# SSM loops with fill work by halves, and the attention's output projection begun behind the last chunk

## The reference, cut to what matters

```python
seg = a_t[..., :, None] - a_t[..., None, :]
decay = jnp.exp(jnp.where(tril, seg, -jnp.inf))
cb = jnp.einsum('bclgn,bcsgn->bcgls', cm, bm)
y_diag = jnp.einsum('bcgls,bcghls,bcsghp->bclghp', cb, decay, xdt)
chunk_states = jnp.einsum('bclgn,bclgh,bclghp->bcghpn', bm, decay_to_end, xdt)
_, prev = lax.scan(carry_step, init, (chunk_states, chunk_decay))   # state before each chunk
y_off = jnp.einsum('bclgn,bcghpn,bclgh->bclghp', cm, prev, jnp.exp(a_cum))
...
y = y + xs * d_skip;  y = y * silu(z);  y = normalize(y per group) * ssm_norm_g
branch_att = att @ w_o_att
branch_ssd = y @ w_o_ssd
merged = sigmoid(g_att) * branch_att + sigmoid(g_ssd) * branch_ssd
return merged @ w_out
```

## Time and profile before

| | us |
|---|---|
| median of 3 runs | 2543.91 (2539.17 to 2546.9) |
| the profiled execution | 2542.98 |
| its span in the profile | 2541.3 |
| TensorE busy in it | 2383.3 |
| TensorE's mean granted clock, share of full | 0.979 |

### The profile page before, as it was taken

The page is one execution under the profiler, slowest core; times in us unless marked ns, Lnnn a source line. Parts: engine busy times, 40 slices in busy tenths (PEclk is TensorE's granted clock), DMA queues, the critical chain, the costliest instruction groups (busy, mean ns, idle before and its releaser), DMA issues.

```text
span 2541.3 us, 31932 instructions
## 1 busy us (share of the span) xinstructions
PE 2383.3 (94%) x12062; PEld 1950.0 (77%) x12062; DVE 1371.9 (54%) x1971; ACT 724.1 (28%) x1371; POOL 858.5 (34%) x353
## 2 busy tenths in 40 slices
PE   3999999997998999999999799999799999999997
PEld 3966878874656888888877688888688888888885
DVE  4249999964656266574655565654523232232316
ACT  5153121005651233434255210024511121211112
POOL 1221332216771352533444233335222333332221
PEclk9999999998999999999999899999999999999998
DMA  7110342216652113131230533333211111111103
GB/s 260 34 34 34 111 171 99 91 42 203 198 174 71 34 59 125 39 120 59 68 107 22 215 136 108 124 132 136 81 50 50 50 50 50 39 43 50 50 33 132
DMA packets 145737, 233.92 MB, mean 92 GB/s; under 512 B 8068, under 2 KB 111844, under 8 KB 144612
## 3 DMA queue, kind: packets, MB, share of 16 engines
q1 hardware_dynamic: 121952, 173.45, 21.0%
q10 hardware_dynamic: 23684, 59.06, 6.0%
HBM read 180.06 MB, written 52.43 MB: 91 GB/s over the span
## 4 chain that ended last, share of the span: by engine, by line
PE 85%; DVE 8%; ACT 3%; issue 2%; DMA 1%; POOL 0%; ACTq 0%; SPq 0%; DVEq 0%
PE ps L634 83%; DVE c_out L1799 2%; PE ps L838 1%; DVE probT L1742 1%; DVE mod_sum L1587 1%; DVE c_out L1797 0%; DMA ada_raw<-in_ada_w_dram 0%; PE ps L921 0%; DVE c_out L1801 0%; DVE x_tm L1969 0%; DVE zy L1845 0%; DMA x_d<-x_tm 0%; ACT decay L1437 0%; DVE x_tm L1906 0%; ACT zy L1370 0%
## 5 line engine op out<-in xcount | busy, mean ns | idle before, releaser
L634 PE MATMUL ps<-a_hi,w_hi 128*128 128x512 f32 x1728 | 679.7, 393 | 11.5 <-DVE a_lo L1852 5.6
L634 PE MATMUL ps<-a_lo,w_hi 128*128 128x512 f32 x1728 | 675.2, 391 | 0.0
L568 POOL CAST w_hi<-raw 128x2048 fp32r<-128x2048 f32 x90 | 176.3, 1959 | 1326.5 <-PE ps L634 1014.4
L634 PE MATMUL ps<-a_hi,w_lo 128*128 128x512 f32 x1728 | 545.0, 391 | 0.0
L570 POOL TENSOR_TENSOR w_lo<-raw,w_hi 128x2048 fp32r<-128x2048 f32 x90 | 429.9, 4777 | 7.2
L1931 DVE TENSOR_TENSOR x_tm<-x_tm,ps 128x1024 f32<-128x1024 f32 x120 | 146.5, 1221 | 453.1 <-PE ps L634 453.1
L634 PEld LDWEIGHTS ps<-a_hi,w_hi 128*128 128x128 f32 x1728 | 326.6, 189 | 81.7 <-issue 7.8
L634 PEld LDWEIGHTS ps<-a_lo,w_hi 128*128 128x128 f32 x1728 | 326.5, 189 | 67.7 <-issue 0.7
L634 PEld LDWEIGHTS ps<-a_hi,w_lo 128*128 128x128 f32 x1728 | 325.7, 188 | 68.2
L634 PE MATMUL ps<-w_hi,a_hi 128*128 128x256 f32 (+1 forms) x896 | 259.6, 290 | 5.0 <-ACT row L1488 2.0
L634 PE MATMUL ps<-w_lo,a_hi 128*128 128x256 f32 (+1 forms) x896 | 254.7, 284 | 0.0
(11 more groups left out here) (249 smaller groups left out, 3162.9 us busy)
## 6 DMA issues: line engine op xcount, KB each, us to landing
raw<-in_w_in_dram SPq DMA_DIRECT2D x35, 1024.0 KB, 5.3
ada_raw<-in_ada_w_dram SPq DMA_DIRECT2D x16, 1024.0 KB, 8.8
raw<-in_w_up_dram SPq DMA_DIRECT2D x16, 1024.0 KB, 5.7
raw<-in_w_down_dram SPq DMA_DIRECT2D x16, 1024.0 KB, 4.9
gates<-gate_d SPq DMA_DIRECT2D x12, 1024.0 KB, 5.0
act_raw<-acts_d ACTq DMA_DIRECT2D x20, 512.0 KB, 5.8
ada<-in_ada_w_dram SPq DMA_DIRECT2D x8, 1024.0 KB, 20.5
acts_d<-decay ACTq DMA_DIRECT2D x16, 512.0 KB, 2.6
```

The source lines that it names most:

```text
L568: nc.gpsimd.tensor_copy(hi, src).then_inc(hi_made, 1)
L634: return nc.tensor.matmul(o, a, b, start=start, stop=stop)
```

## The change

The fill work is placed by halves. `fill_parts(g, k)` gives the halves behind chunk `k`: two behind chunks 0 to 5 and one behind 6 and 7 in group 0; two behind chunks 0 to 3 and one behind 4 to 7 in groups 1 and 2; two behind chunks 0 to 5 and none behind 6 and 7 in group 3. In every group one half now stands between `segments(0)` and `segments(1)`, and one behind `segments(1)`. The state product of each group's last chunk is left out; `mix_done` of that chunk comes from the product `state, c_fm`.

The first output block moves ahead of the four turns of y in the last group. It ends in banks 5, 0, 1 and 2 (`FIRST_OUT`), and the turns use the pairs 3-4 and 6-7. The buffers `act_raw`, `gates` and `gated` get other addresses, so that SP can load the attention tiles 0 and 1 as soon as the last `segments` is done, and tiles 2 and 3 when the last fill tiles are stored. ScalarE rounds tiles 0 to 3 inside the last loop and tiles 4 to 7 behind the root, ahead of the copies of the turned y; DVE makes `a_lo` of tiles 0 and 1 ahead of y of the last chunk, 2 and 3 behind it, 4 behind the variance, and 5 to 7 behind the 8 scalings. POOL's split of the next weight block waits for the last y and no longer for the scalings. `acc` is cleared in two parts, and DVE's loop over the first two turns of output blocks is written out. SP's load of `x_in` waits for other semaphores.

```diff
-    act_raw = [place(f"act_raw{i}", [P, SEQ], F32, R2 + (0, 4, 48, 52)[i] * K) for i in range(4)]
-    gates = [place(f"gates{i}", [P, 2, SEQ], F32, R2 + (8 + 8 * i) * K) for i in range(2)]
-    gated = [place(f"gated{i}", [P, 512], F32, R2 + (24 + 2 * i) * K) for i in range(2)]
+    act_raw = [place(f"act_raw{i}", [P, SEQ], F32, R2 + (12352, 16448, 0, 4128)[i]) for i in range(4)]
+    gates = [place(f"gates{i}", [P, 2, SEQ], F32, R2 + (48 * K, 20544)[i]) for i in range(2)]
+    gated = [place(f"gated{i}", [P, 512], F32, R2 + 8256 + 2 * i * K) for i in range(2)]
...
-        def fill_places(g):
-
-            return {k: k for k in range(NT)} if g == 0 else {0: 2, 1: 3, 3: 4, 4: 5, 5: 6, 6: 7}
+        def fill_parts(g, k):
+
+            first = 2 if g == 0 else 4
+            each = (2, 2, 2, 2, 2, 2, 1, 1) if g == 0 else (2, 2, 2, 2, 1, 1, 1, 1) if g + 1 < NG else (2, 2, 2, 2, 2, 2, 0, 0)
+            n = first + sum(each[0:k])
+            return range(n, n + each[k])
...
+        FIRST_OUT = (5, 0, 1, 2)
...
                 load(N_O + j, cols(w_o_att[0], j * WC))
                 if j == 1:
 
+                    sp.wait_ge(seg_done, NG * NT)
+                    for k in range(4):
+                        if k >= 2:
+                            sp.wait_ge(fill_stored[k - 2], 64 * NG)
+                        sp.dma_start(act_raw[k][:, :], acts_d[k]).then_inc(act_in[k], 16)
+
                     sp.wait_ge(y_ready, NG * NT)
-                    for b in range(2):
-                        sp.wait_ge(fill_stored[b], 64 * NG)
-                    for k in range(4):
-                        sp.dma_start(act_raw[k][:, :], acts_d[k]).then_inc(act_in[k], 16)
-
-                    for m in range(2):
-                        sp.wait_ge(y_stored[m], 16 * 2 * NG)
                     load_gates(0, 0)
                     load_gates(1, 2)
...
-                    sp.wait_ge(gate_used, 16 * 3)
-                    sp.wait_ge(act_split, 3 * KT)
+                    sp.wait_ge(act_split, 4 * KT - 1)
...
-            pool.wait_ge(gn_ready, NG * NT)
+            pool.wait_ge(y_ready, NG * NT)
             with pool.Fori(0, (N_ALL - N_O) // 2 - 1) as i:
...
+            def y_banks(g, f):
+                return (4, 6)[f % 2] if g + 1 < NG else (3, 6)[f % 2]
...
+                j = 1 if g else 0
                 segments(0)
+                fill(g, j, 0)
                 segments(1)
-                if g:
-                    fill(g, 1, 0)
-                    fill(g, 1, 1)
+                fill(g, j, 1)
                 pe.wait_ge(tile_out, g * 5 + 5)
-                places = fill_places(g)
...
-                        mm(ps[:, 3, :], c_fm[:, k * P:(k + 1) * P], state[:, :, :].rearrange("p h d -> p (h d)"),
-                           start=True, stop=True)
-                    mm(ps[:, 6, :], b_tm[:, k, :], xde[k % 2][:, :, :].rearrange("p h d -> p (h d)"),
-                       start=True, stop=True).then_inc(mix_done, 1)
+                        mixed = mm(ps[:, 3, :], c_fm[:, k * P:(k + 1) * P], state[:, :, :].rearrange("p h d -> p (h d)"),
+                                   start=True, stop=True)
+                        if k == NT - 1:
+                            mixed.then_inc(mix_done, 1)
+                    if k < NT - 1:
+                        mm(ps[:, 6, :], b_tm[:, k, :], xde[k % 2][:, :, :].rearrange("p h d -> p (h d)"),
+                           start=True, stop=True).then_inc(mix_done, 1)
                     if k + 2 < NT:
                         segments(k + 2)
-                    if k in places:
-                        fill(g, places[k], 0)
-                        fill(g, places[k], 1)
-
-            for f in range(4):
-                y_turn(NG - 1, f)
+                    for part in fill_parts(g, k):
+                        fill(g, *divmod(part, 2))
...
-                last = fm_block(n, j % 2, extra=0 if turn is None else turn * 2, act_ready=ready, act_used=used)
+                last = fm_block(n, j % 2, extra=0 if turn is None else turn * 2, act_ready=ready, act_used=used,
+                                banks=FIRST_OUT if (o, j) == (0, 0) else None)
                 last.then_inc(w_used[n % 2], 1)
 
-            for j in range(4):
+            pe.wait_ge(decay_done, NG * NT)
+            pe.wait_ge(fill_out, NG * 8)
+            pe.wait_ge(y_ready, NG * NT - 1)
+            out_block(N_O, 0, 0)
+            for f in range(4):
+                y_turn(NG - 1, f)
+            pe.wait_ge(yt_out, NG * 4)
+            pe.wait_ge(gate_used, 1)
+            for j in range(1, 4):
                 out_block(N_O + j, j, 0)
...
+            def act_load(k, tile):
+                act.dma_start(act_raw[k % 4][:, :], acts_d[bass.ds(tile, 1)].rearrange("a p s -> p (a s)")).then_inc(act_in[k % 4], 16)
+
+            def first_acts(tiles):
+                for k in tiles:
+                    act.wait_ge(act_in[k % 4], 16 * (k // 4 + 1))
+                    nc.scalar.copy(a_hi[:, k, :], act_raw[k % 4][:, :]).then_inc(hi_copied, 1)
+                    if 1 <= k < KT - 3:
+                        act.wait_ge(act_split, k)
+                        act_load(k + 3, k + 3)
...
                 def squares_of(k):
                     act.wait_ge(y_ready, g * NT + (k + 1))
-                    nc.scalar.activation(c_out[k % 2][:, 0:DG], zy[:, k, :], ACT.Square,
+                    nc.scalar.activation(c_out[0][:, k % 2 * DG:k % 2 * DG + DG], zy[:, k, :], ACT.Square,
...
-                    if k == 1 and g:
-                        fill_evac(g, 1)
-                    if k - 2 in places:
-                        fill_evac(g, places[k - 2])
+                    if k == 1:
+                        fill_evac(g, 1 if g else 0)
+                    for part in fill_parts(g, k - 2) if k >= 2 else ():
+                        if part % 2:
+                            fill_evac(g, part // 2)
+                    if g == NG - 1 and k >= NT - 1:
+                        first_acts({NT - 1: (0, 1), NT: (2,), NT + 1: (3,)}[k])
                     if k >= 2:
                         squares_of(k - 2)
                 act.wait_ge(gn_var, g + 1)
                 nc.scalar.activation(stat[:, 96:104], stat[:, 96:104], ACT.Sqrt).then_inc(gn_root, 1)
+            first_acts(range(4, KT))
             for f in range(4):
                 y_evac(NG - 1, f)
...
                 for k in range(NT):
                     if k + 1 < NT:
                         mix_in(k + 1)
+                    if g == NG - 1 and k == NT - 1:
+                        act_lo(0, tiles=(0, 1))
                     dve.wait_ge(mix_done, g * NT + (k + 1))
...
+                if g == NG - 1:
+                    act_lo(0, tiles=(2, 3))
                 dve.wait_ge(gn_squares, g * NT + NT)
                 ve.tensor_scalar(stat[:, 96:104], stat[:, 96:104], 1.0 / DG, EPS, ALU.mult, ALU.add).then_inc(gn_var, 1)
+                if g == NG - 1:
+                    act_lo(0, tiles=(4,))
...
 
+            act_lo(0, tiles=range(5, KT))
+            V.link(ve.memset(acc[:, 0:KT // 2, :], 0.0))
+            for i in range(2):
                 for j in range(3):
-                    gate_block(N_O + j, j, i)
+                    gate_block(N_O + j, j, i, FIRST_OUT if (i, j) == (0, 0) else None)
+                    if (i, j) == (0, 0):
+                        dve.wait_ge(yt_done, NG * 4)
+                        V.link(ve.memset(acc[:, KT // 2:KT, :], 0.0))
                 act_lo(i * 8 + 8)
                 gate_block(N_O + 3, 3, i)
-                V.leave(2)
```

More of the change, by code:

```diff
@@ L634, in mm, with fm_block @@
                 return nc.tensor.matmul(o, a, b, start=start, stop=stop)
-            def fm_block(n, group, extra=0, act_ready=None, act_used=None):
+            def fm_block(n, group, extra=0, act_ready=None, act_used=None, banks=None):
                 s = n % 2
+                banks = banks or range(4 * group, 4 * group + 4)
                 w_wait(n, extra)
@@ L646, in fm_block @@
                         for q in range(2):
-                            o = ps[:, 4 * group + 2 * m + q, :]
+                            o = ps[:, banks[2 * m + q], :]
                             r = slice(q * 512, q * 512 + 512)
@@ L651, in fm_block @@
                         for q in range(2):
-                            last = mm(ps[:, 4 * group + 2 * m + q, :], wl, a_hi[:, k, q * 512:q * 512 + 512],
+                            last = mm(ps[:, banks[2 * m + q], :], wl, a_hi[:, k, q * 512:q * 512 + 512],
                                       stop=(k == KT - 1))
@@ L857, in y_turn @@
                 for t in range(NT):
-                    last = nc.tensor.transpose(ps[:, 4 + 2 * (f % 2) + t // 4, (t % 4) * P:(t % 4 + 1) * P],
+                    last = nc.tensor.transpose(ps[:, y_banks(g, f) + t // 4, (t % 4) * P:(t % 4 + 1) * P],
                                                zy[:, t, f * P:(f + 1) * P], ident[:, :])
@@ L1447, in _ @@
```

(22 more changed lines are left out.)

10 lines of the change are left out of this document (3 added, 7 removed).

## The result

The median of the changed kernel is 2502.8 us (2501.4 to 2504.7), against 2542.7 for the kernel before: 0.984 of it, with a 95% interval of 0.9826 to 0.986. The forecast was 2504.5. In the profiled executions the span fell from 2541.3 to 2501.8 us, by 39.5, against a sum of 39.6.

A forecast was written before the change was run, and what follows sets the result against it. TensorE, busy 2383.3 of 2541.3 us, was taken as the bound, through its waits and low clock. Terms 11.2 + 6.8 - 2.3 + 3.4 + 3.5 + 11 + 6 = 39.6 us gave 2504.5 us, range 2495 to 2525.

The forecast's parts named there:

- The half ahead of `segments(1)`: Half a fill tile in each group's 4.1 us gap while ScalarE's exponentials finish: 4 x 2.8 = 11.2 us gained.
- The rest waits: What stays of each group's 3.0 us wait for the exponentials once the gap holds a half: 1.0 us each.
- Chunk 2's waits: Three waits for y behind chunk 2 of groups 1 to 3, covered by two halves there: 6.8 us gained.
- New wait behind chunk 4: Groups 1 and 2, where one half doesn't cover y held by POOL's split: 1.2 us each, 2.3 us lost.
- Rival 3: DVE bounds the loop: POOL's subtraction delays all ten singly covered chunks, kernel slower, 2553 us; chance 0.04.
- Last state products: Leaving out the state product of each group's last chunk on TensorE: 4 x 0.86 = 3.4 us gained.
- `turn_tile`: Its waits for DVE's convolutions go, as a half behind the last chunk in groups 1 and 2 gives lead: 3.5 us gained.
- The clock: TensorE's half-clock stretches behind waits mostly go: 11 us gained of 17.5, bounds 0 and 17.5.
- rival 1: The clock doesn't come back: remaining short waits in groups and tail are followed by half clock too, 2520 us; chance 0.18.
- The tail: From chunk 5's end in group 3 to the second output block, first block ahead of the turns: 6 us (5.9) gained.
- TensorE waits 2.3 and 1.8 us: First output block: two waits ahead of tiles 4 and 5, from POOL's subtraction holding DVE's `a_lo` and then the scalings.
- Rival 2: First output block starves, each tile a load late through ScalarE's list: tail -10 instead of +6, 2520.5 us; chance 0.13.

The follow-up runs named there:

- the moved half: Changed kernel with POOL's split behind the scalings and two more turned-tile buffers, one half of group 3's fill put behind chunk 6 instead of 5: 2498.3 us, 0.9810.

## Why the prediction was right, point by point

The groups' lengths can be closed with the prediction's own terms; the clock is what remains.

- **The half ahead of `segments(1)`**: 2.95 us each inside the gap of 4.1, as said (11.2 forecast, 11.8 measured). The rest waits came to 4.0 us for the forecast 4 x 1.0, three of them 0.7 or 0.8 and one, in group 3, 1.8. Chunk 0 was nowhere late.
- **Chunk 2's waits**: 6.8 forecast, 6.8 gone. **New wait behind chunk 4**: 1.2 forecast, 0.92 measured, twice; no other chunk with single cover waited. Rival 3 needed 4 us in each of ten chunks and is refuted.
- **Last state products**: 0.86 each forecast; 0.9 to 1.0 where they were put back. **`turn_tile`**: 3.5 forecast, 3.3 gained, and the wait returns as soon as chunk 7 has no fill.
- **The clock** was the term with the widest bounds (0 to 17.5, taken at 11), and it was under-sized. What it gave back is a remainder here. Group 0 gained 7.9 us: 2.95 is the half, 0.9 the product, 4.1 remain. Group 1: 6.5 - 2.95 - 2.2 + 0.92 - 0.9 = 1.4. Group 2, with its 1.5 of `turn_tile`: 8.2 - 2.95 - 2.2 + 0.92 - 0.9 - 1.5 = 1.6. Group 3: 20.1, less 2.95, 2.4 for chunk 2, 1.8 for `turn_tile`, 0.9 and the tail's 5.7, leaves 6.4. In all 13.5. The experiment without the early half shows the price of a single wait of 3.0 us: some 2.5 us of clock behind it. Two such waits fewer in group 3 (3.0 and 2.4) give 5 of its 6.4. As a check, the half clock behind the waits in the trace before, read from stretches of 10 us, lacks 4.3, 1.7, 1.7 and 2.9 us behind the four waits for the exponentials and 2.9 behind chunk 2's wait of group 3, and 1.7 more at `turn_tile`, which is 15.2 in all, near the 13.5. The last one the prediction overlooked: a wait of 2.01 us, shorter than the two of 2.2 that it held against rival 1, had half clock behind it (0.66 over the 5 us from 1309.9; the turns took 1.97 us, and 1.09 in group 2).

```profile
...
1309.93 1.97 PE L921 MATMUL ps<-ident,c_out 128*128 128x128 f32 x8 [2.01 <-ACT c_out L1354]
...
```

- **The tail**: 59.0 - 52.4 - 0.9 = 5.7 against 5.9 forecast. The wait ahead of chunk 7's `state, c_fm` was 2.64 for 2.7, the turns took 7.7 for 7.4. By this milestone the size is right, but one step inside was not: "TensorE waits 2.3 and 1.8 us" ahead of tiles 4 and 5. The prediction let the split hold `a_lo` of tile 4; it held the variance, one step sooner, which it had taken as free. Through root and rounding this made tile 4 later (its `a_lo` was ready at 31.8 on the prediction's scale, where it was put at 29), and one wait of 3.54 us took the place of two: behind it tile 4 ran at half clock, 4.5 us instead of 2.7, and this covered the scalings, so that tile 5's `a_lo`, ready at some 1387.9, was there when its products began at 1387.97. The block ended 2.9 us later than forecast (28.9 us long: 21.8 of products, 3.5 of wait, 3.6 of low clock). These 3.6 us the prediction had at nothing; the 3 us that it allowed stood for low clock behind the turns. There 1.7 us came too, but behind the second block's start, so the 52.4 doesn't hold them. With them the tail gives 4.0 instead of 5.9.
- **Rival 1** falls in the groups, as the experiment without the early half shows. In the tail its mechanism was there: each of the three waits (2.64, 3.54 and 2.82 us) had half clock behind it, 5.0 us in all by the stretches, where the prediction allowed 3.
- **Rival 2**, a block that waits at each tile, is refuted in the changed kernel: one wait. It isn't far, though: with the half behind chunk 6 three tiles waited.
- **Not in the sum**: 2.0 us more ahead of the loops, 1.5 of it a later landing of `v_d`, in code that the change leaves alone. The 1.2 us less gained behind the second block's start are the tail's 1.7 of half clock, less 0.5 gained. Against these stands the clock's surplus of 2.5. That the sum met the span within 0.1 us is luck of about 3 us in both directions; what holds is that no single term was off by more than that. The step from the sum to the time was written 0.2 too high: 2501.7 + 1.7 + 0.9 is 2504.3.

The Trainium skill, "VectorE: DVE Perf Modes", section "Mode 2×_2P — use both read ports for one tensor", says that an instruction with one source in SBUF can take both of VectorE's read ports, for fp32 too. Together with the rule cited in the prediction this makes an operation of one input, such as the variance, as exposed to GpSimd as `a_lo`. The trace agrees by 4.58 against 0.17 us: this very small operation paid the whole rest of POOL's instruction.

## What to carry to other kernels

A wait of TensorE costs more than its length where low clock follows it, so half a tile of fill in each of two gaps was worth more here than a whole one in the first. Before you let POOL begin earlier, list every DVE operation that lies beside its work, the tiny ones that others wait for above all: here a split some 8 us sooner cost 3.3 us. When a wait appears after an edit, look at what its releaser was doing before you blame the edit: the 2.50 us behind the moved half came from DVE held by POOL, and a like one (2.27 us) came without the edit too.

## What the runs showed of the hardware

- An operation of 128x8 numbers took 4.58 us instead of 0.17 beside POOL's subtraction, and ended with it. Operations with two SBUF inputs were held likewise: a pair of `a_lo` took 4.05 us instead of 2.35 beside POOL's rounding (1371.49 to 1374.02), and the last `a_lo` 5.22 and 5.23 us instead of 1.22 in the two traces in which it began behind POOL's subtraction.
- The length of a wait alone didn't tell whether half clock followed it. All waits of 3.0 us in the groups had it (0.73 over 11 us behind one). For `state, c_fm` behind a wait for y, where 1.10 us is the full clock, the traces give: 1.10 us after waits of 2.19 or 2.20 us, four times; 2.04 or 2.05 us after waits of 2.38 us, three times; anything from 1.10 to 2.04 after the wait of 2.64 us in the tail, in eleven executions. Other places don't fit a limit between 2.2 and 2.4 us: `turn_tile` ran at half clock behind a wait of 2.01 us (1.97 us for 8 turns instead of 1.09), the clock was 0.72 over 6 us behind a wait of 1.73 us in one trace, and with the half behind chunk 6 the clock stayed at 1.00 behind waits of 2.13 and 2.50 us. In the changed kernel's groups the waits of 0.7 to 1.8 us brought none.
